# Second block: gate and up-projection units with stationary activations, the merge done by tokens and turned

## What is computed

```python
h = rmsnorm_2(x, norm_mix[l])
proj = h @ w_in[l]
(qa, ka, va, qb, kc, vc, ksl, vsl, kw, vw, g_nsa, g_a, g_b) = jnp.split(proj, IN_OFFSETS, axis=-1)
y_a = swa_sink_attention(...)          # 8 heads of 64
y_b = nsa_attention(...)               # 8 heads of 64: compressed, selected, window branches
merged = sigmoid(g_a) * (y_a @ w_up_a[l]) + sigmoid(g_b) * (y_b @ w_up_b[l])
x = x + merged @ w_out[l]
```

## Time and profile before

| | |
|---|---|
| median of three runs | 839.55 us (839.41 to 840.27) |
| span of the profiled execution, first to last instruction | 837.8 us |
| TensorE busy | 828.7 us, 99% |
| VectorE busy | 639.9 us, 76% |
| ScalarE busy | 447.6 us, 53% |

### The profile page before, as it was taken

How to read it: one execution, slowest core, us unless ns; L and a number is a source line. 1 busy time by engine, 2 the same in 40 slices (tenths; PEclk the granted TensorE clock), 3 DMA queues, 4 the chain that set the end, 5 groups by cost and what they waited for, 6 DMA issues and landing times.

```text
span 837.8 us, 13770 instructions
## 1 busy us (share of the span) xinstructions
PE 828.7 (99%) x5313; PEld 731.7 (87%) x5315; DVE 639.9 (76%) x791; ACT 447.6 (53%) x564; POOL 88.1 (11%) x93
## 2 busy tenths in 40 slices
PE   8999999999999999999999999999999999999996
PEld 6888888888988888888888899999998988888895
DVE  5786766667967587676667779897775898998897
ACT  6555444546324554544444756784425655665664
POOL 2000000004450300000000326000003000000001
PEclk9999999999999999999999999999999999999999
DMA  8876566564854467656656585567446455466541
GB/s 242 317 240 210 184 196 205 167 201 159 243 158 144 151 206 259 239 180 197 204 194 169 132 220 156 132 172 223 159 154 198 141 201 201 150 200 212 189 175 51
DMA packets 119970, 157.73 MB, mean 188 GB/s; under 512 B 4429, under 2 KB 104173, under 8 KB 119805
## 3 DMA queue, kind: packets, MB, share of 16 engines
q1 hardware_dynamic: 117292, 150.56, 56.9%
q0 software_dynamic: 1392, 5.34, 1.9%
q10 hardware_dynamic: 1248, 1.32, 0.5%
HBM read 154.42 MB, written 1.07 MB: 186 GB/s over the span
## 4 chain that ended last, share of the span: by engine, by line
PE 98%; DMA 1%; POOL 0%; ACTq 0%; DVE 0%; issue 0%; POOLq 0%; DVEq 0%
PE wk L1722 30%; PE acc L1844 20%; PE wk L1691 18%; PE wk L1730 16%; PE acc L1821 7%; PE wk L2171 1%; PE acc L2135 1%; PE acc L1738 1%; DMA x<-in_x 1%; PE acc L1691 1%; PE acc L2150 1%; PE wk L2233 1%; PE wk L2235 0%; PE acc L1857 0%; PE acc L2196 0%; PE wk L2031 0%
## 5 line engine op out<-in xcount | busy, mean ns | idle before, releaser
L1722 PE MATMUL wk<-xhl,w_hi 128*128 128x512 f32 x1104 | 268.9, 391 | 0.0
L1040 DVE TENSOR_TENSOR w_lo<-raw,w_hi 128x2048 fp32r<-128x2048 f32 x83 | 190.0, 2289 | 63.9 <-ACT w_hi L493 62.8
L1722 PEld LDWEIGHTS wk<-xhl,w_hi 128*128 128x128 f32 x1104 | 202.5, 188 | 38.9 <-issue 0.2
L493 ACT ACTIVATE w_hi<-raw 128x2048 fp32r<-128x2048 f32 x83 | 158.0, 1904 | 0.0
L1730 PEld LDWEIGHTS wk<-xhl,w_lo 128*128 128x128 f32 x1104 | 145.5, 191 | 8.0
L1730 PE MATMUL wk<-xhl,w_lo 128*128 128x256 f32 x1104 | 147.9, 282 | 0.0
L486 ACT ACTIVATE w_hi<-raw 128x2048 fp32r<-128x2048 f32 x55 | 104.6, 1910 | 51.6 <-PE wk L1691 29.9
L1023 DVE TENSOR_TENSOR w_lo<-raw,w_hi 128x2048 fp32r<-128x2048 f32 x48 | 110.2, 2300 | 21.3 <-ACT w_hi L486 21.1
L1844 PE MATMUL acc<-w_hi,hhl 128*128 128x512 f32 x480 | 119.4, 391 | 0.0
L1691 PE MATMUL wk<-xhl,w_hi 128*128 128x256 f32 x608 | 108.6, 286 | 0.0
L1844 PEld LDWEIGHTS acc<-w_hi,hhl 128*128 128x128 f32 x480 | 88.2, 188 | 17.1
(11 more groups left out here) (267 smaller groups left out, 965.6 us busy)
## 6 DMA issues: line engine op xcount, KB each, us to landing
raw<-in_ffn_w SPq DMA_DIRECT2D x65, 1024.0 KB, 5.4
raw<-in_w_in SPq DMA_DIRECT2D x24, 1024.0 KB, 6.8
raw<-in_w_ffn_in SPq DMA_DIRECT2D x22, 1024.0 KB, 5.1
raw<-in_w_ffn_out SPq DMA_DIRECT2D x11, 1024.0 KB, 4.9
raw<-in_w_out SPq DMA_DIRECT2D x8, 1024.0 KB, 4.9
arena<-bias_scratch POOLq DMA_DIRECT2D x4, 512.0 KB, 6.6
raw<-in_w_in SPq DMA_DIRECT2D x4, 512.0 KB, 7.1
raw<-in_cmp_w_k SPq DMA_DIRECT2D x2, 1024.0 KB, 5.5
```

The source lines that it names most:

```text
L493: nc.scalar.activation(w_hi[:, s], raw[:, s], ACT.Copy).then_inc(hi_done, 1)
L1040: nc.vector.tensor_tensor(w_lo[:, s], raw[:, s], w_hi[:, s].bitcast(F32), ALU.subtract) \
L1722: mm = nc.tensor.matmul(bank, wh[:, c, cols], xhl[:, c].rearrange("p n t -> p (n t)"), start=c == 0, stop=False, skip_group_check=True)
```

## The change

Gate units now hold 512 weight columns by four chunks (`GATES`, the SP queue loads `w2[:, k0:k0+4, c0:c0+512]`). `gate_tile` keeps 128 tokens of activations stationary and streams 512 weight columns, 12 matmuls per token half; two units make one sum of 128 tokens x 512 features, in banks 0 and 1 of `wk`, one for each token half. ScalarE takes the tanh straight out of PSUM (`gate_row`) with the tokens' half 1/rms as a per-partition scale (`half_root`, one small new operation on VectorE); the eight multiplications on VectorE go. Attention's values use bank 2 alone, for both token halves in turn, with a wait of TensorE for `y_taken` at each change of half, and the compression units use bank 3. The up units likewise stream 512 columns past stationary y, in two token halves; gates, products and their sum then have tokens on the partitions, and 16 transposes (`turn_merged`, two groups of eight) bring the sum into PSUM with features on the partitions, from where ScalarE and VectorE split it as before. The first group stands between the two halves of the fourth up unit, the second after the first output unit.

The diff, cut to its core:

```diff
@@ -62,2 +62,2 @@
-IN2_COLS = (512, 0, 256, 1280, None, 768, None, 1024, 2072, None, 2328, None, 2584, None, 2840, None,
-            3096, 3352, 3608, 3864)
+IN2_COLS = (512, 0, 256, 1280, None, 768, None, 1024)
+GATE_COL = 2072
@@ -67 +67 @@
-GA, CW, GB = (8, 10, 12, 14), (9, 11, 13, 15), (16, 17, 18, 19)
+CW, GATES = (9, 11, 13, 15), (8, 10, 12, 14, 16, 17, 18, 19)
...
@@ -262,0 +263 @@
+        half_root = sb("half_root", [P, 2])
@@ -278,0 +280,3 @@
+        def merged_chunks(j):
+            return wk[:, 2 - 2 * j:4 - 2 * j].rearrange("p b (h t) -> p (b h) t", t=T)
+
...
@@ -447,0 +453,5 @@
+                elif m in GATES:
+                    n = GATES.index(m)
+                    c0, k0 = GATE_COL + 512 * (n // 2), 4 * (n % 2)
+                    unit(U_IN2 + m, w2[:, k0:k0 + 4, c0:c0 + 512], 4)
+                    continue
@@ -705,4 +715,9 @@
-            def gate_tanhs(j, n_out):
-                act.wait_ge(proj2, n_out)
-                buf = (ga if j < 4 else gb)[:, 2 * (j % 4):2 * (j % 4) + 2]
-                nc.scalar.activation(buf, buf, ACT.Tanh, scale=0.5).then_inc(ga_tanh, 1)
+            def gate_row(pair, tt):
+
+                if tt:
+                    act.wait_ge(unit_done, U_IN2 + GATES[2 * pair + 1] + 1)
+                else:
+                    act.wait_ge(gate_mm, pair + 1)
+                c0 = 512 * (pair % 2)
+                nc.scalar.activation((ga if pair < 2 else gb)[:, tt, c0:c0 + 512], wk[:, tt], ACT.Tanh,
+                                     scale=half_root[:, tt:tt + 1]).then_inc(gate_out, 1)
@@ -714,0 +730,6 @@
+                    if half and m in GATES[1::2]:
+                        if m == GATES[1]:
+                            act.wait_ge(half_ready, 1)
+                        gate_row(GATES.index(m) // 2, 0)
+                    if half == 0 and m - 1 in GATES[1::2]:
+                        gate_row(GATES.index(m - 1) // 2, 1)
...
@@ -770,2 +787,2 @@
-                act.wait_ge(merged, j + 1)
-                nc.scalar.activation(xh[:, 4 * j:4 * j + 4], ga[:, 4 * j:4 * j + 4], ACT.Copy).then_inc(merged_hi, 1)
+                act.wait_ge(merged_turned, j + 1)
+                nc.scalar.activation(xh[:, 4 * j:4 * j + 4], merged_chunks(j), ACT.Copy).then_inc(merged_hi, 1)
@@ -1101,0 +1119 @@
+                nc.vector.tensor_scalar(half_root[:], both_r[:, 2:4], 0.5, None, ALU.mult).then_inc(half_ready, 1)
...
@@ -1411 +1425 @@
-                bank = wk[:, 3 - b].rearrange("p (h d) -> p h d", d=HD)
+                bank = wk[:, 2].rearrange("p (h d) -> p h d", d=HD)
...
@@ -1500 +1514 @@
-                elif m - 1 not in CW and m not in CW:
+                elif m <= GATES[0]:
@@ -1520,2 +1533,0 @@
-                    if m in CW and half == 0:
-                        proj_2(m - 1)
@@ -1538 +1549,0 @@
-            proj_2(19)
@@ -1552,5 +1563,4 @@
-                dve.wait_ge(ga_tanh, 2 * m + 2)
-                buf = (ga if m < 2 else gb)[:, 4 * (m % 2):4 * (m % 2) + 4]
-                b0 = 2 - 2 * (m % 2)
-                banks = wk[:, b0:b0 + 2].rearrange("p b (h t) -> p (b h) t", t=T)
-                nc.vector.scalar_tensor_tensor(out=buf, in0=buf, scalar=1.0, in1=banks, op0=ALU.add,
+                dve.wait_ge(gate_out, 2 * m + 2)
+                cols = slice(512 * (m % 2), 512 * (m % 2 + 1))
+                buf, b0 = (ga if m < 2 else gb)[:, :, cols], 2 - 2 * (m % 2)
+                nc.vector.scalar_tensor_tensor(out=buf, in0=buf, scalar=1.0, in1=wk[:, b0:b0 + 2], op0=ALU.add,
@@ -1560,2 +1570 @@
-                    both = ga[:, 4 * (m - 2):4 * (m - 2) + 4]
-                    nc.vector.tensor_tensor(both, both, buf, ALU.add).then_inc(merged, 1)
+                    nc.vector.tensor_tensor(ga[:, :, cols], ga[:, :, cols], buf, ALU.add).then_inc(merged, 1)
@@ -1573 +1582 @@
-                nc.vector.tensor_tensor(xl[:, cols], ga[:, cols], xh[:, cols].bitcast(F32), ALU.subtract) \
+                nc.vector.tensor_tensor(xl[:, cols], merged_chunks(m - 2), xh[:, cols].bitcast(F32), ALU.subtract) \
@@ -2161,2 +2170,2 @@
-                        if r and w in (0, 4):
-                            pe.wait_ge(y_taken, 2 * r - (w == 0))
+                        if s and w in (0, 4):
+                            pe.wait_ge(y_taken, 2 * r + (w == 4))
@@ -2171 +2180 @@
-                                    mm = nc.tensor.matmul(wk[t0:t0 + HD, 3 - b, cols],
+                                    mm = nc.tensor.matmul(wk[t0:t0 + HD, 2, cols],
@@ -2190,0 +2200,13 @@
+            def gate_tile(n, slot, tt):
+
+                pair, closes = divmod(n, 2)
+                if not closes:
+                    if pair:
+                        pe.wait_ge(gate_out, 2 * pair - 1 + tt)
+                    else:
+                        pe.wait_ge(proj2, M_ROWS + 1 + tt)
+                mm = tok_tile(slot, tt, wk[:, tt], 4 * closes)
+                if closes and tt == 0:
+                    mm.then_inc(gate_mm, 1)
+                return mm
+
...
@@ -2211 +2231 @@
-                    pe.wait_ge(proj2, 8)
+                    pe.wait_ge(proj2, M_ROWS + 1)
@@ -2214 +2234 @@
-                    nc.tensor.matmul(wk[:, 1], zeros[:, 0:P], zeros[:], start=True, stop=False,
+                    nc.tensor.matmul(wk[:, 3], zeros[:, 0:P], zeros[:], start=True, stop=False,
...
@@ -2242,0 +2257,2 @@
+                    elif m in GATES:
+                        mm = gate_tile(GATES.index(m), s, half)
...
@@ -2308,2 +2324,4 @@
-            def up(m, tiles=range(4)):
-                b0 = 2 - 2 * (m % 2)
+            def up(m, tiles=range(2)):
+
+                slot = (U_UP + m) % SLOTS
+                wh, wl = k_n(w_hi[:, slot], 4), k_n(w_lo[:, slot], 4)
@@ -2311,4 +2329,7 @@
-                for t in tiles:
-                    mm = col_tile((U_UP + m) % SLOTS, t, wk[:, b0 + t // 2, (t % 2) * T:(t % 2 + 1) * T],
-                                  4, mh, ml, 4 * (m // 2))
-                if 3 in tiles:
+                for tt in tiles:
+                    rows = slice(tt * P, (tt + 1) * P)
+                    for c in range(4):
+                        f = 4 * (m // 2) + c
+                        mm = passes(wk[:, 2 - 2 * (m % 2) + tt], ((mh[:, f, rows], wh[:, c]), (mh[:, f, rows], wl[:, c]),
+                                                                  (ml[:, f, rows], wh[:, c])), c == 0, c == 3)
+                if 1 in tiles:
@@ -2316,0 +2338,9 @@
+            def turn_merged(j):
+
+                pe.wait_ge(merged, j + 1)
+                for c in range(4):
+                    for tt in range(2):
+                        cols = slice(512 * j + c * P, 512 * j + (c + 1) * P)
+                        mm = nc.tensor.transpose(merged_chunks(j)[:, c, tt * P:(tt + 1) * P], ga[:, tt, cols], ident)
+                mm.then_inc(merged_turned, 1)
+
@@ -2318 +2348,2 @@
-            up(0, range(0, 3))
+            pe.wait_ge(hid_taken, 1)
+            up(0, (0,))
@@ -2322,2 +2353,2 @@
-            up(0, range(3, 4))
-            pe.wait_ge(proj2, 16)
+            up(0, (1,))
+            pe.wait_ge(gate_out, 8)
@@ -2329 +2360,3 @@
-            up(3)
+            up(3, (0,))
+            turn_merged(0)
+            up(3, (1,))
@@ -2336,0 +2370,2 @@
+                if m == 0:
+                    turn_merged(1)
```

More of the change, by code:

```diff
@@ L232, in build @@
         bias = carve(0, 16, T)
-        ga, gb = carve(16, DC, T), carve(24, DC, T)
+        ga, gb = carve(16, 2, D), carve(24, 2, D)
         blk = carve(24, 2, 16, 32)
@@ L322, in build @@
             sem(n) for n in ("proj2", "value_turned", "kz_zero", "kz_direct", "kz_ready"))
-        ga_tanh = sem("ga_tanh")
+        gate_mm, half_ready, gate_out = (sem(n) for n in ("gate_mm", "half_ready", "gate_out"))
+        merged_turned = sem("merged_turned")
         score_mm, logit_out, neg_max, exp_out, prob_turned, prob_t_out, pv_mm, y_taken = (
@@ L721, in _ @@
                         act.wait_ge(unit_done, U_IN2 + CW[3] + 1)
-                        nc.scalar.activation(hid_rows, wk[0:64, 1], ACT.Copy).then_inc(hid_rows_out, 1)
+                        nc.scalar.activation(hid_rows, wk[0:64, 3], ACT.Copy).then_inc(hid_rows_out, 1)
                     if half == 0:
@@ L737, in _ @@
                         nc.scalar.activation(gates[:], gates[:], ACT.Tanh, scale=0.5).then_inc(gate_tanhed, 1)
-                    if half == 1 and m - 1 in GA:
-                        gate_tanhs(GA.index(m - 1), 9 + GA.index(m - 1))
                     if k == 8:
@@ L757, in _ @@
                         nc.scalar.activation(prob_ct, k_n(acc[:, 3, 0:T], 2), ACT.Copy).then_inc(cprob_t, 1)
-                    if half == 1 and m - 1 in GB:
-                        gate_tanhs(4 + GB.index(m - 1), 13 + GB.index(m - 1))
+            gate_row(3, 1)
             hi_next = U_UP + 2
             hi(hi_next)
-            gate_tanhs(7, 16)
             y_hi_part(2)
@@ L1349, in proj_2 @@
                     dst = qa_s[:, 2 * M_QA.index(m):2 * M_QA.index(m) + 2]
```

(14 more changed lines are left out.)

8 lines of the change are left out of this document (removed).

## The result

The changed kernel takes 844.86 us (median of five runs, 842.99 to 845.22) against 839.55 us before (here the median of five runs, 839.41 to 840.27), so the medians differ by 5.3 us. The ratio is put at 1.0056, with a 95% interval of 1.0045 to 1.0067: 4.7 us slower, 3.8 to 5.6 by the interval. The span of its profiled execution is 843.0 us, 5.2 us more than before. The forecast was 843.0 us and slower.

The account below looks back on a forecast made before the run. The prediction took TensorE, busy 99% of the span, as the bound. Gates -2.1, values' bank +4.3 and up units with merge +1.2 gave +3.4 us on the median of 839.55: 843.0 us, range 841.0 to 845.0.

Parts of the forecast that it names:

- rival 3: Attention positions 15 and 17: the waits pass on, each costing up to a microsecond, 845.0 us; chance 0.05.
- The values' bank: Attention's value matmuls: TensorE waits for VectorE's takes at positions 9, 11, 15 and 17, +4.3 us (3.9 to 4.8).
- nothing on DVE ahead of that take is removed: Position 9: no VectorE work before the take goes, so it still ends at 529.04 and TensorE waits 2.18 us.
- The clock: Behind the waits at positions 9 and 11: granted clock taken as staying at 1.00, at no cost.
- rival 4: Behind the waits at positions 9 and 11: idle time lowers TensorE's clock until the next position, 849.8 to 856.7 us; chance 0.03.
- The gates: Gate units, sixteen halves with 512 columns in place of 256: 0.13 us saved each, -2.1 us (-1.9 to -2.5).
- The up units and the merge: Eight up halves -1.05 us, sixteen transposes +1.74, two small waits of 0.23 and 0.25: net +1.2 us (0.6 to 1.9).
- Both small waits: Up units: TensorE waits 0.23 us before turn_y(2) and 0.25 us for the banks that up(3) needs.
- rivals 1 to 3: First: both takes in time, 838.6 us, chance 0.05; second: one wait swallowed, 841.0 us, 0.07; third: as under rival 3.
- The start-to-start distance of the two value groups: Sign in the profile: TensorE's two idle times of about 2 us before value matmuls, about 8.9 us apart.

Follow-up runs that it names:

- takes_early: The changed kernel with VectorE's two takes of branch 0, and the sink's small operations, moved ahead: 840.1 us, ratio 1.0001.
- bank_only: The kernel before with attention's values in one bank for both token halves and the change's waits, gates and up units as they were: 845.6 us, ratio 1.0068.
- warm_fill: The changed kernel with nine matmuls of zeros ahead of the values of position 9, filling the first wait: 845.86 us, ratio 1.0062.
- warm_both: The changed kernel with nine matmuls of zeros ahead of the values of position 9 and of position 11: 843.52 us, ratio 1.0044.
- best2: The changed kernel with branch 0's takes, the eighth unit's multiplication and the second up unit's eviction earlier, y_b's turns behind the whole first up unit: 839.2 us, ratio 0.9986.

## Why the prediction was right, and where it fell short

Sign and range held; the forecast of +3.4 was 1.9 us short of the measured +5.3. That the range held is in part luck: the bounds of the terms end at 844.4, below the measured 844.86, and the range reached 845.0 only by rival 3, which did not come. By its terms, for the profiled execution:

**The values' bank: right, to within 0.2 us.** PE's start at position 9 was forecast at 529.14 and is 529.14; the hundredth is luck, as the two traces differ by 0.05 at position 5 already. The waits, counted as in the forecast from when PE was due, were 2.22, 2.05, 0.05 and 0.13 (forecast 2.18, 2.03, 0.02 and 0.1), in sum 4.45 against 4.3. The step "nothing on DVE ahead of that take is removed" was the right one to look at: takes_early shows that the place of the takes decides, and the multiplications that leave DVE behind them give no relief.

**The clock: the step that failed.** The forecast took the time behind each wait at full speed; "rival 4" had the mechanism, at a chance of 0.03. It came in part: behind one wait and not both, and for 1.46 us, not for the 6.86 us to the next position. With 1.46 us more the forecast would have been 844.5. The reason given against it, that no row with an idle time of 2 us existed to test it, was no reason for a small chance: there was nothing for or against, and a wait of this length had just been forecast. bank_only, warm_fill and warm_both show that the idle time brings the fall, with the old gate units too, that it can come behind either wait, and that it costs about 1.5 us each time (1.46 in the changed kernel, 1.5 in bank_only, 1.6 in warm_fill).

**The gates: right.** Eleven of the sixteen gate halves lie behind the values of position 17, where no wait of PE shows any more. From there to the scores against the compressed keys it was 45.04 us (553.74 to 598.78 below) and is 43.61 (559.03 to 602.64): 1.43 us less, 0.13 per half as forecast, 2.1 over sixteen.

```profile
602.64 1.13 PE L2320 MATMUL acc<-arena 64*128 64x256 f32 x8
```

best2, which has no long waits, agrees. Start of the values at position 5, and of the scores against the compressed keys, before and in best2:

```profile
509.67 1.15 PE L2171 MATMUL wk<-arena 128*64 128x64 f32 x32
...
598.78 1.13 PE L2304 MATMUL acc<-arena 64*128 64x256 f32 x8
```

```profile
510.04 1.15 PE L2183 MATMUL wk<-arena 128*64 128x64 f32 x32
...
597.34 1.13 PE L2323 MATMUL acc<-arena 64*128 64x256 f32 x8
```

The stretch went from 89.11 to 87.30 us: -1.81, with some 0.2 of small waits at positions 15 and 17 still in it, so -2.0. In the changed kernel the same two rows are 509.62 and 602.64, +3.91; less 4.45 for the waits and 1.46 for the clock leaves -2.0 for the gates. Forecast -2.1, bounds -1.9 to -2.5.

By the Trainium skill, TensorE: Matmul & The Clock Gate, section Back-to-back issue gap, the gain would have been 12 pairs of 2.5 ns, 0.03 us per half unit (an estimate from that page's table, which the page gives for isolated matmuls). Measured are 2.0 to 2.1 us over sixteen halves, 0.13 each, and the measurement decides.

**The up units and the merge: right.** Span 5.2 less 3.86 (602.64 against 598.78) is +1.34; forecast 1.2, bounds 0.6 to 1.9. Both small waits are there (0.18 + 0.35 for 0.23 + 0.25), with a third of 0.12 in the output projection that was not forecast. The transposes took 0.80 and 0.79 us per group and the matmul behind each 0.09 more, 1.77 in all against 1.74 taken from the earlier trace rows. With eight halves at -0.13 these parts make 1.4. best2, where the first two waits are gone, has +0.74 (its span is 0.7 shorter than before, 1.81 of which it had won by 597.34, and it started 0.37 later), against 1.74 - 1.05 = 0.69 by the forecast's prices.

The sum of the measured terms is 4.45 + 1.46 - 2.1 + 1.34 = 5.2 us, the difference of the spans. The last term is what the span leaves, so the check lies in the first three: 3.8 us against the 3.9 that the stretch behind position 5 grew. The rivals 1 to 3 did not come: no take was in time, no wait was swallowed, positions 15 and 17 stayed small. The start-to-start distance of the two value groups was said to be about 8.9 us (the prediction's own starts, 529.14 and 537.90, give 8.76) and is 10.26; the 1.5 more is the clock.

## What to carry to other kernels

When a buffer is given to another use, look for the instruction that empties it, and set its end against the time at which the bound engine comes back, instruction by instruction; where it is late, move that instruction ahead in its own engine's order, and then look at what it has pushed back. Price an idle time of the array by its length plus a stretch of half clock behind it (here 2.0 to 2.2 us, and 1.5 more for one of two). Halving the number of matmuls by doubling their columns won 0.13 us per 24 matmuls here, 3.1 us over the 24 halves of gates and up units; the 16 transposes that the layout then needs, 0.11 us each, gave 1.8 of that back.

## What the runs showed of the hardware that was not expected

A wait of 2 us is enough to bring the granted clock to 0.50, but not every one does. Of the two waits, some 10 us apart, the first did in the changed kernel and in bank_only, and the second where the first was filled (warm_fill). The length alone does not decide: the second wait brought the fall in warm_fill at 1.97 us of idle time and not in the changed kernel at 1.99. An idle time of 0.56 us (takes_early) had no such effect. What decides was not tried further, and each kernel has one trace; it stays open. The changed kernel's fastest run, 842.99 us at a mean granted clock of 0.998 where the others have 0.995 to 0.997, would fit an execution without the fall, but it has no trace here.

Matmuls of zeros in the waits kept the clock at 1.00 (warm_both); nine of them past 512 columns took 2.1 us (2.12 at 526.94 there).
